# Gathered rows of experts 2 to 8 turned in 32x32 blocks by VectorE from a relaid staging tensor, in place of 128x128 turns by TensorE

## The reference

```python
def swiglu(h, w_gu, w_down):
    g, u = jnp.split(h @ w_gu, 2, axis=-1)
    return (jax.nn.silu(g) * u) @ w_down

def moe_swiglu(h, w_router, b_router, w_gu, w_down):
    ...
    top_vals, top_idx = lax.top_k(logits, TOP_K)
    wts = jax.nn.softmax(top_vals, axis=-1)
    combine = jnp.sum(jax.nn.one_hot(top_idx, N_EXPERTS, dtype=jnp.float32) * wts[..., None], axis=1)
    ...
    for e in range(N_EXPERTS):
        y = y + combine[:, e:e + 1] * swiglu(xf, w_gu[e], w_down[e])
    return y.reshape(B, S, D)
```

## Time and profile before

| | before |
|---|---|
| median of three runs | 1447.14 us |
| span of the profiled execution, first to last instruction | 1446.1 us |
| TensorE busy, share of the span | 1437.5 us, 99% |
| VectorE busy | 1162.2 us, 80% |
| ScalarE busy | 962.2 us, 67% |
| GpSimd busy | 44.7 us, 3% |
| DMA, mean over the span | 287 GB/s |
| eight experts | from about 689 us to the end |

### The profile page before, as it was taken

How to read it: one execution, slowest core, us unless ns; L and a number is a source line. 1 busy time by engine, 2 the same in 40 slices (tenths; PEclk the granted TensorE clock), 3 DMA queues, 4 the chain that set the end, 5 groups by cost and what they waited for, 6 DMA issues and landing times.

```text
span 1446.1 us, 19518 instructions
## 1 busy us (share of the span) xinstructions
PE 1437.5 (99%) x6835; PEld 1186.4 (82%) x6835; DVE 1162.2 (80%) x1148; ACT 962.2 (67%) x1052; POOL 44.7 (3%) x53
## 2 busy tenths in 40 slices
PE   9999999999999999999999999999999999999998
PEld 7888888888888888888888888888888888888876
DVE  6987756665547977657998999989999999899987
ACT  6676654444345677744777777777777777777775
POOL 2000003000000000000200000000000000000300
PEclk9999999999999999999999999999999999999999
DMA  9463348955465462448899999999999999999995
GB/s 338 157 234 117 119 153 305 327 182 182 146 233 169 167 226 98 146 149 297 303 388 388 389 357 396 387 362 393 369 395 397 356 401 368 389 392 350 367 374 212
DMA packets 212571, 414.93 MB, mean 287 GB/s; under 512 B 14188, under 2 KB 55528, under 8 KB 212504
## 3 DMA queue, kind: packets, MB, share of 16 engines
q1 hardware_dynamic: 206488, 393.42, 75.2%
q0 software_dynamic: 4976, 16.97, 3.5%
q10 hardware_dynamic: 1040, 3.68, 0.6%
HBM read 398.20 MB, written 15.81 MB: 286 GB/s over the span
## 4 chain that ended last, share of the span: by engine, by line
PE 97%; DMA 2%; DVE 1%; ACT 0%; issue 0%; SPq 0%; POOL 0%; ACTq 0%; POOLq 0%
PE ps L538 88%; DMA raw_low<-in_moe_w_gu 2%; PE ps L1098 1%; PE ps L806 1%; PE ps L961 1%; PE ps L939 1%; PE ps L948 1%; PE ps L919 1%; PE ps L854 1%; PE ps L938 0%; PE ps L888 0%; PE ps L1079 0%; PE ps L932 0%; ACT w_hi L503 0%; PE ps L917 0%; PE ps L827 0%
## 5 line engine op out<-in xcount | busy, mean ns | idle before, releaser
L508 DVE TENSOR_TENSOR w_lo<-raw,w_hi 128x2048 fp32r<-128x2048 f32 (+2 forms) x240 | 511.3, 2140 | 145.0 <-ACT w_hi L503 141.8
L503 ACT ACTIVATE w_hi<-raw 128x2048 fp32r<-128x2048 f32 (+2 forms) x240 | 431.6, 1800 | 212.4 <-PE ps L538 196.3
L538 PE MATMUL ps<-w_hi,act_hi 128*128 128x512 f32 (+1 forms) x1264 | 332.7, 393 | 0.8 <-ACT act_hi L1262 0.5
L538 PE MATMUL ps<-w_hi,act_lo 128*128 128x512 f32 (+1 forms) x1264 | 328.9, 388 | 0.0
L538 PE MATMUL ps<-w_lo,act_hi 128*128 128x512 f32 (+1 forms) x1264 | 325.2, 388 | 0.3 <-DVE w_lo L508 0.2
L538 PEld LDWEIGHTS ps<-w_lo,act_hi 128*128 128x128 f32 x1264 | 235.4, 188 | 49.4 <-DVE w_lo L508 1.1
L538 PEld LDWEIGHTS ps<-w_hi,act_lo 128*128 128x128 f32 x1264 | 234.9, 188 | 48.1
L538 PEld LDWEIGHTS ps<-w_hi,act_hi 128*128 128x128 f32 x1264 | 231.0, 188 | 46.7 <-ACT act_hi L1262 1.3
L503 ACT ACTIVATE w_hi<-raw_more 128x2048 fp32r<-128x2048 f32 x96 | 170.7, 1778 | 65.4 <-PE ps L538 64.1
L508 DVE TENSOR_TENSOR w_lo<-raw_more,w_hi 128x2048 fp32r<-128x2048 f32 x96 | 201.1, 2110 | 14.3 <-ACT w_hi L503 12.8
L508 DVE TENSOR_TENSOR w_lo<-raw_low,w_hi 128x2048 fp32r<-128x2048 f32 (+1 forms) x64 | 128.9, 2022 | 13.5 <-ACT w_hi L503 12.6
(11 more groups left out here) (289 smaller groups left out, 1285.3 us busy)
## 6 DMA issues: line engine op xcount, KB each, us to landing
raw<-in_moe_w_gu SPq DMA_DIRECT2D x192, 512.0 KB, 9.8
raw_more<-in_moe_w_gu SPq DMA_DIRECT2D x96, 512.0 KB, 10.3
raw<-in_w_in SPq DMA_DIRECT2D x72, 512.0 KB, 4.5
raw_low<-in_moe_w_gu SPq DMA_DIRECT2D x64, 512.0 KB, 9.9
raw_more<-in_moe_w_down SPq DMA_DIRECT2D x64, 512.0 KB, 6.6
raw<-in_dense_w_gu SPq DMA_DIRECT2D x44, 512.0 KB, 4.9
raw_low<-in_moe_w_down SPq DMA_DIRECT2D x32, 512.0 KB, 8.0
raw<-in_moe_w_down SPq DMA_DIRECT2D x32, 512.0 KB, 5.7
```

Source lines behind the costliest of these rows:

```text
L503: nc.scalar.activation(w_hi[:, self.split_slot(j), 0:n], self.raw(j)[:, 0:n], ACT.Copy).then_inc(self.hi, 1)
L508: nc.vector.tensor_tensor(w_lo[:, c, 0:n], self.raw(j)[:, 0:n], w_hi[:, c, 0:n].bitcast(F32), ALU.subtract).then_inc(self.lo, 1)
L538: return nc.tensor.matmul(dst, a, b, start=start and n == 0, stop=stop and n == 2)
```

## The change

- `xs` now holds the rows relaid: partition 32g + i holds, for b = 0 to 3, the channels of column group g of slot 32b + i. The load of 128 whole rows becomes four loads of 32 x 4 x 256 numbers, and a fifth of 128 x 8 numbers brings the routing weights into a tensor of their own, `xw`.
- For each row group to come out right, `row_lists` writes `xn` with its channels in another order. It does so in eight instructions of 256 columns in place of two of 1024.
- VectorE turns the whole of `xs` with one transpose in 32x32 blocks (`gather_turn`), behind its split in step d = 4. The result, `x_t`, lies in the first half of `xn`.
- ScalarE and VectorE make `act_hi` and `act_lo` from `x_t` in SBUF and no longer from PSUM. VectorE does its halves at d = 6 and 8, no longer at 5 and 7; ScalarE stays at 5 and 7.
- TensorE's eight transposes of each of the seven experts are gone, with their waits. `TURNS` falls from 8 to 6.
- Expert 0 and the arithmetic of all matmuls stay as they are. The second pass is changed in the same way.

```diff
-    TURNS = EGS + 2
+    TURNS = EGS
...
-        xs = sb("xs", [P, D + E], F32, ffn)
+        xs = sb("xs", [P, TT * 2, S], F32, ffn)
+        xw = sb("xw", [P, E], F32, ffn)
...
+        def gathers(q, e):
+            return e + 1 if q else e
+        def slot_columns(v):
+            return v.rearrange("p (k g c) -> p g k c", k=KD, g=4)
+        def slot_rows(v):
+            return v.rearrange("p (g k c) -> p g k c", k=KD, g=4)
+        x_t = xn[:, 0, 0:D].rearrange("p (k s) -> p k s", k=KD)
...
                 if q or not isinstance(e, int) or e > 1:
                     sp.wait_ge(z["slot_read"], e)
-                sp.dma_start(xs[:], x_rows[e, q]).then_inc(z["xs_landed"], 16)
+                    sp.wait_ge(z["xs_turned"], gathers(q, e - 1))
+                slots = x_rows[e, q].rearrange("(b i) d -> i b d", b=4)
+                for g in range(4):
+                    sp.dma_start(xs[32 * g:32 * g + 32, :, :], slots[:, :, g * S:(g + 1) * S]).then_inc(z["xs_landed"], 16)
+                sp.dma_start(xw[:], x_rows[e, q, :, D:D + E]).then_inc(z["xw_landed"], 16)
...
-                        if not last and d in (4, 6):
-                            half = (d - 4) // 2
-                            if not half:
-                                pe.wait_ge(z["xs_landed"], 16 * (e + 2))
-                            pe.wait_ge(z[f"eturn_free{half}"], turns_read(e, EGS))
-                            gather(half)
...
                 def gather_part(e, half):
-                    act.wait_ge(z["eturn_done"], gather_turn_no(e, half) + 1)
-                    copy(act_hi[:, 4 * half:4 * half + 4, 0:P], ps[:, 4 + half, :].rearrange("p (k s) -> p k s", k=4)
-                         ).then_inc(z["eturn_hi"], 1)
+                    act.wait_ge(z["xs_turned"], gathers(q, e))
+                    k = slice(4 * half, 4 * half + 4)
+                    copy(act_hi[:, k, 0:P], x_t[:, k, :]).then_inc(z["x_hi"], 1)
...
                 for t in range(TT):
-                    op = stt(xn[:, t, 0:D], xres[:, t, :], small[:, 2 + t:3 + t], gain_row[:], ALU.mult, ALU.mult)
+                    for g in range(4):
+                        op = stt(slot_rows(xn[:, t, 0:D])[:, g], slot_columns(xres[:, t, :])[:, g], small[:, 2 + t:3 + t],
+                                 slot_columns(gain_row[:])[:, g], ALU.mult, ALU.mult)
...
+                def gather_turn(e):
+                    dve.wait_ge(z["xs_landed"], 64 * gathers(q, e))
+                    if q or not is_first(e - 1):
+                        dve.wait_ge(z["x_lo"], 2 * gathers(q, e) - 2)
+                    nc.vector.transpose(x_t.rearrange("p k (b i) -> p b k i", b=4),
+                                        xs[:].rearrange("p b (k c) -> p b k c", k=KD)).then_inc(z["xs_turned"], 1)
...
-                        if not last and d in (5, 7):
-                            gather_part(e + 1, (d - 5) // 2)
+                        if not last and d == 4:
+                            gather_turn(e + 1)
+                        if not last and d in (6, 8):
+                            gather_part(e + 1, (d - 6) // 2)
```

More of the change, by code:

```diff
@@ L1073, in moe_pass @@
                 z = pass_sems[q]
[L1075 to L1080, removed]
                 def first_gather(pair):
@@ L1085, in first_gather @@
                         dst = ps[:, FIRST_BANK[pair], k * P:(k + 1) * P]
[L1086 to L1090, removed]
+                        for t in range(1 if pair < 2 and not k else 0, TT):
+                            mm = nc.tensor.matmul(dst, xres[:, t, c:c + P], pick[:, t, :], start=t == 0, stop=t == TT - 1)
                     mm.then_inc(z["first_turned"], 1)
@@ L1155, in body @@
                             pe.wait_ge(z[f"gu_free{j % 2}"], strips_read(e, j))
-                        if j == 0 and first:
+                        if j == 0 and first and not q:
                             pe.wait_ge(z["first_hi"], k0 // 2 + 1)
                         elif j == 0 and k0 % 4 == 0:
-                            pe.wait_ge(z["eturn_hi"], gather_turn_no(e, k0 // 4) + 1)
+                            pe.wait_ge(z["x_hi"], 2 * gathers(q, e) + k0 // 4 - 1)
                         ch, cl = r.take(pe, e, c)
@@ L1163, in body @@
                         for p in range(3):
-                            if p == 1 and j == 0 and first:
+                            if p == 1 and j == 0 and first and not q:
                                 pe.wait_ge(z["first_lo"], k0 // 2 + 1)
                             elif p == 1 and j == 0 and k0 % 4 == 0:
-                                pe.wait_ge(z[f"eturn_free{k0 // 4}"], turns_read(e, 0))
+                                pe.wait_ge(z["x_lo"], 2 * gathers(q, e) + k0 // 4 - 1)
                             if p == 2:
@@ L1238, in moe_pass @@
                     pe.wait_ge(pick_ready, 2)
-                for pair in range(4):
-                    first_gather(pair)
+                    for pair in range(4):
+                        first_gather(pair)
                 body(0, False)
@@ L1590, in body @@
                         act.dma_start(y_rows[e], y_sb[:]).then_inc(z["y_stored"], 16)
-                for pair in range(4):
-                    first_part(pair)
+                if q:
+                    for half in range(2):
+                        gather_part(0, half)
+                else:
+                    for pair in range(4):
+                        first_part(pair)
                 body(0, False)
@@ L2006, in turn_part @@
                        ehid_hi[:, 4 * j:4 * j + n, :].bitcast(F32), ALU.subtract).then_inc(z[f"eturn_free{j % 2}"], 1)
+                def gather_turn(e):
[4 more added lines that the diff above has]
+                                        xs[:].rearrange("p b (k c) -> p b k c", k=KD)).then_inc(z["xs_turned"], 1)
                 def gather_part(e, half):
[L2009 to L2012, removed]
+                    dve.wait_ge(z["x_hi"], 2 * gathers(q, e) + half - 1)
+                    k = slice(4 * half, 4 * half + 4)
+                    tt(act_lo[:, k, 0:P], x_t[:, k, :], act_hi[:, k, 0:P].bitcast(F32), ALU.subtract).then_inc(z["x_lo"], 1)
                 def first_part():
@@ L2082, in body @@
                         scattered(e + 1)
-                if not q:
+                if q:
+                    gather_turn(0)
+                    for half in range(2):
+                        gather_part(0, half)
+                else:
                     moe_ring.split_lo(dve, 0, LEAD - 1)
-                first_part()
-                if not q:
+                    first_part()
                     row_lists()
```

36 lines of the change are left out of this document (15 added, 21 removed).

## The result

The changed kernel takes **1460.86 us** (median of 4 runs, 1458.68 to 1462.24), the kernel before 1447.26 us: ratio 1.0091, 95% interval [1.0079, 1.0103]. It is 13.6 us slower, where 5.1 us faster was forecast. The profiled execution took 1458.68 us with a span of 1456.9 us, 10.8 us more than before.

A forecast was written before the change was run, and what follows sets the result against it. TensorE, busy in 99% of the span, was taken to bound the kernel. Terms: -6.7 + 0 + 0.85 + 0.7 = -5.15 us, so 1447.1 - 5.1 = 1442.0 us; range 1440.2 to 1446.6 us.

The forecast's parts named there:

- What is removed: TensorE's two transpose groups for each of seven experts, in the down part, 0.48 us each: -6.7 us, all on the path.
- VectorE's transpose: In the down part: 1.2 us, hidden up to about 2.0 us, cost 0; piece 10 keeps 0.86 us of reserve.
- Both rivals on the transpose: Eight times a 128-column instruction: 2.75 us, time 1447.3 us, chance 0.12. Four passes over fp32: 4.4 us, time 1458.8 us, chance 0.06.
- Their break-even: The transpose length from which the change was said to end up slower than before: about 3.2 us.
- The row lists: Eight instructions of 256 columns for two of 1024, on the path before TensorE's w_lo: +0.85 us, between 0.4 and 1.5.
- The prediction's second estimate: For the row lists, from the skill's fixed 75 ns per instruction: 6 x 0.075 = 0.45 us.
- The crowded place: At the end, while GpSimd gathers: the ring's reserve is used up, so late weights cost +0.7 us, between 0 and 5.8.
- The row loads: Five DMAs for one on SyncE, 1.3 us more issue time: nothing with ring reserve, at most a few tenths per expert.
- The prediction's own sign against it: In the profile after, ScalarE waiting for weights before the last expert would make the prediction wrong.
- The rival "the loads can't follow": Less time and more small pieces empty the ring; TensorE stands at the crowded place: 4 us more, 1446, chance 0.09.

The follow-up runs named there:

- e1: The changed kernel with the rows in one load of 128 partitions with 4 KB each, not relaid: 1442.04 us.
- e6: The changed kernel with one row load of all 128 partitions in 512 pieces of 1 KB, not relaid: 1441.62 us.
- e11: The changed kernel with two row loads of 64 partitions by 4 KB, both into partitions 32 to 95: 1441.49 us.
- e16: e9 with SyncE's loop over experts 2 to 7 written out in Python: 1441.27 us.
- e2: The changed kernel with four row loads by columns, each 256 columns of all 128 partitions, not relaid: 1446.16 us.
- e9: The changed kernel with four loads of whole 4 KB rows, load g into partitions g, g+4, g+8 and so on, not relaid: 1445.41 us.
- e13: e1 with eight already-met waits added ahead of each of down pieces 0 to 5 in SyncE's loop, no DMA added: 1443.46 us.
- e12: The changed kernel with two row loads of whole 4 KB rows, partitions 0 to 63 and then 64 to 127, not relaid: 1442.64 us.
- e14: The changed kernel with SyncE's loop over experts 2 to 7 written out in Python, row loads as in the change: 1445.38 us.
- e10: The changed kernel with two row loads of 64 partitions by 4 KB, both into partitions 0 to 63: 1448.98 us.
- e3: The changed kernel with four row loads of 32 neighbouring partitions each, in whole 4 KB rows, not relaid: 1458.85 us.
- e8: The changed kernel with its relaid loads spread on SyncE's queue, one each ahead of down pieces 2, 3, 4 and 5: 1462.16 us.
- e5: The changed kernel with its relaid row loads and the routing weights' load issued by ScalarE in place of SyncE: 1441.08 us.
- e15: e5 with 48 already-met waits added to SyncE's loop: 1453.5 us.
- e4: The changed kernel with the same relaid result, its four loads cut by slot block, each into all 128 partitions: 1463.47 us.
- e7: The kernel before, with its row load of experts 2 to 8 cut into four of 32 partitions with whole rows: 1457.42 us.

## Why the prediction was wrong

Two causes are at work: a *dip*, the transfer rate that falls at the row loads, and a *pause*, SyncE's wait for code at the turn of its loop. In one table: the median, and SyncE's waits for slots in five turns (862 to 1325 us).

| | code kept or in sequence | code fetched in each turn |
|---|---|---|
| no dip (379 to 406 GB/s, 828 to 840 us) | e1 1442.0 us, 123.5; e6 1441.6 us, 118.4; e11 1441.5 us, 110.6; e16 1441.3 us, 164.3 | e2 1446.2 us, 52.0; e9 1445.4 us, 50.6; e13 1443.5 us, 56.0 |
| dip on SyncE's queue (304 to 329 GB/s) | e12 1442.6 us, 71.3; e14 1445.4 us, 107.1; e10 1449.0 us, 62.3 | after 1460.9 us, 14.2; e3 1458.9 us, 16.5; e8 1462.2 us, 2.5 |
| loads on ScalarE's queue (340 and 345 GB/s) | e5 1441.1 us, 139.8 | e15 1453.5 us, 32.0 |

Against e1, the pause alone costs 1.4 to 4.1 us and the dip alone 0.6 to 6.9 us; together they cost 17 to 20, more than the sum. The distances between the experts' readings of their routing weights show why. In e2, e9, e10, e12, e13 and e14, each with one cause, all distances but the last are 92.4 or 92.5 us as in e1. What these kernels lose stands in the last one, beside GpSimd's gathers: 94.4 us in e1, 96.6 in e12 and e13, 98.3 in e9, 98.5 in e2 and e14, 101.7 in e10. With both causes the distances before it grow too, from the fourth on in the change and e3, from the third in e8. e4 and e7 are left out of the table, e4 for its four engines and e7 for its longer period; e7 has both causes.

The windows above give the size, as an estimate. At the rates that e1 and e12 reach in the four stretches, an expert could be fed 407 x 12 + 410 x 24 + 398 x 24 + 388 x 32.45 = 36.9 MB in 92.45 us; it needs the 35.6 MB that e1 moves. 1.3 MB, 3 us of transfer, are to spare. The row loads lose (407 - 291) x 12 = 1.4 MB in e12. The pause in e13 loses, against 405 GB/s, (60 + 223) x 4 = 1.1 MB. One loss is about made good in each expert; two leave an estimated 1.2 MB, 3 us, unpaid. The periods of the changed kernel once its reserve was gone were 2.3, 3.0 and 3.4 us over 92.45, and 10.0 us in the last, where e1 has 1.9. Why the dip alone costs so unequally there (e12, e14 and e10 have 304 to 306 GB/s alike) is open.

By the steps of the prediction:

- *What is removed*, -6.7 us: right. The pairs are 4.08 and 4.11 us apart, the period in e1 is 92.45 us. This holds in the changed kernel for its first three distances; behind them, late weights hide it.
- *VectorE's transpose*, 1.2 us, hidden, 0.86 us left at piece 10: right, 1.24 and 0.89 us. The 2.5 us estimated from the Trainium skill's "VectorE: DVE Perf Modes" was not borne out; "Vector Engine (DVE) Microarchitecture Reference", 3.8, was near, with 1239 ns for 1024 columns. Both rivals on the transpose fall. (Their break-even was off: the change would have been level at 2.0 + 5.1 / 7 = 2.7 us of transpose; 3.2 us is where it would have been clearly slower.)
- *The row lists*, +0.85 us: right, about 0.8. Eight instructions took 3.25 us where two took 2.48, and TensorE waits 1.24 us where it waited 0.45. The prediction's second estimate, 0.45 us, was too small: each added instruction cost 0.13 us.

```profile
694.87 3.25 DVE L1999 SCALAR_TENSOR_TENSOR xn<-xres,small,gain_row 128x256 f32<-128x256 f32 x8
...
700.38 0.77 PEld L539 LDWEIGHTS ps<-w_lo,act_hi 128*128 128x128 f32 x4 [1.24 <-DVE w_lo L509]
```

- *The crowded place*, +0.7 us: not borne out in e1. From 1340 to 1400 us TensorE is idle 0.06 us in e1's trace and 0.57 us in the one before. e1's profiled execution took 1441.29 us, which is the forecast without this term; its median of 1442.04 us meets the whole forecast partly by luck.
- *The row loads*, "Cost: nothing while the ring has a reserve, at most a few tenths of DMA time in each expert": this step failed, by 19 us. I priced four loads by their issue time (they start within 2.1 us, a little more than assumed) and their bytes. Neither mattered. What I left out was where the bytes land (32 neighbouring partitions) and how many instructions stand in SyncE's loop. The prediction's own sign against it came true: ScalarE waits for weights before the last expert, as the rows from 1212.25 to 1305.70 us show. I also took SyncE's 33.1 us of waiting for slots as a reserve of that size. It says that the queue is ahead, not by how many bytes it could catch up; that was an estimated 3 us of transfer in an expert. The waits don't even order the kernels: e14 has 107.1 us of them and is slower than e12 with 71.3.
- *The rival "the loads can't follow"*, 1446 us at 0.09, named the right resource. It had the cause wrong (less time and small pieces; e6 shows that the pieces cost nothing, e7 that the loss comes without less time) and put the trouble only at the crowded place, so its price was too low by 15 us.

On the partitions, the row is the 291 GB/s of e12 and e9's 392 GB/s in the same stretch. The rule stands in the Trainium skill, "SBUF — State Buffer", Door 1: of 16 ports, partitions 0 to 31 reach eight and 0 to 63 the same eight, 32 to 95 or every fourth all sixteen. The traces agree in all six forms. From 828 to 840 us they show 405 GB/s (whole), 308 (quarters), 379 (every fourth), 306 (0 to 63 twice), 405 (32 to 95 twice) and 304 (halves), and at the worst it is half the rate. 2 us each of the changed kernel, just behind the row loads:

```profile
832.00:834.00 2.00, 2.00 (x11) 1.65 (x10) 1.97 (x4) 1.20 (x2) 0.00 (x0) 1.00 1.16 224
834.00:836.00 2.00, 2.00 (x11) 1.65 (x10) 2.00 (x2) 1.55 (x1) 0.00 (x0) 1.00 1.07 210
```

The fastest kernel that does all of the reference's work is e5, 1441.1 us: 6.4 us below before and 19.8 below the change. It keeps SyncE's loop short, and the rate at its row loads stays at 345 to 358 GB/s. With the loop made long again (e15), 12.4 of the 19.8 us are lost: that part is code. The other 7.4 us stay, so issuing from ScalarE also does something of its own, and the rate falls less there (340 GB/s in e15 against 305 in the change). Why is open; its four loads are issued over 8 us in place of 2. A dip on SyncE's queue leaves a kernel at the edge, as the spreads of e10 and e14 show (10 us each, against 1 us in e1 and e5). Not tried: writing x_rows to memory in an order that one load could bring in relaid, and a shorter loop on SyncE by fewer weight loads.

## What to carry to other kernels

An edit on a DMA queue can have three prices beside its issue time and its bytes: the partitions that it lands in, the number of engines that it spreads over, and the length of the loop that issues it; look at the rows of the instruction queues before and after, even where they say 0.1%. A queue that waits for slots is ahead, but what it can make good is the rate it reaches without waits less the rate that is needed, and two small losses in one round add up against that one sum: each was nearly free alone. When a cure works (another queue), test what else it changed before you name the cause.

## What the runs showed that I had not expected

- SyncE waited 5 to 6 us for code at each turn of its loop, brought on by a few instructions more; TensorE's first longer period in the changed kernel is the fourth.
- Writing the loop out in full took the pause away: 29 or 30 fetches in the whole execution against 53, and 0.9 us at that place.
- Losses that no expert showed came out all at once in the last one, where GpSimd gathers: 98.5 us for the last distance in e14 against 94.4 in e1, with 92.45 us in every one before.
- The row loads in 1 KB pieces (e6, 1441.6 us) cost no more than in 4 KB pieces (e1, 1442.0 us), beside a stream at 400 GB/s.
- VectorE turned 128x1024 fp32 elements in 1239 ns, as fast as it goes over them once (1225 ns).
